# A hybrid convolution, pooling and MLP block on eight cores: layer norm output and MLP input transposed by DMA, Silu from side buffers, three gate products issued first, the last output tile in three column parts

## What is computed

```python
u = rms_norm(h, mix_pre_g)
proj = u @ w_in                                    # 1024 -> 5120
a, gate = split(proj[..., :2048]);  c = a * sigmoid(gate)
c = depthwise_causal_conv(c, dw_kernel, dw_bias)   # width 31
c = layer_norm(c, ln_g, ln_b)                      # over the 1024 channels of a token
y_conv = swish(c) @ w_conv_out
y_pool = pooling_branch(proj[..., 2048:3072])      # trailing means, per-group linear, w_pool_out
g_conv, g_pool = split(sigmoid(proj[..., 3072:]))
merged = g_conv * y_conv + g_pool * y_pool
h = h + rms_norm(merged @ w_o, mix_post_g)
v = rms_norm(h, mlp_pre_g)
v = square(relu(v @ w_ff1)) @ w_ff2                # 1024 -> 4096 -> 1024
h = h + rms_norm(v, mlp_post_g)
```

## Time and profile before

| | us |
|---|---|
| the three timed runs | 979.9, 981.34, 1103.43 |
| their median | 981.34 |
| the profiled execution | 980.87 |
| its span on its slowest core (core 7) | 979.3 |
| spans of all eight cores | 976.0 to 979.3 |

### The profile page before, as it was taken

One profiled execution on the slowest core, in us unless ns is written; L12 is line 12 of the kernel. 1 busy time (PEld: TensorE's weight loads), 2 busy tenths in 40 slices (PEclk: granted clock), 3 DMA queues, 4 the chain that ended last, 5 costly groups with the idle time before them and its releaser, 6 DMA issues.

```text
span 979.3 us, 15429 instructions; the slowest of 8 cores (976.0 to 979.3 us)
## 1 busy us (share of the span) xinstructions
PE 960.4 (98%) x5246; PEld 491.7 (50%) x5246; DVE 413.8 (42%) x671; ACT 338.3 (35%) x606; POOL 34.8 (4%) x50
## 2 busy tenths in 40 slices
PE   5999999999999999999999999999999999999997
PEld 3555666776554544444444444444444444444443
DVE  3464233334558213565555542254323542245222
ACT  3565223112112861464554331034211431034211
POOL 3000000000000000010101000000000000000000
PEclk9999999999999999999999999999999999999999
DMA  9999403656669008739597991340131301330021
GB/s 193 215 218 180 69 1 53 108 93 101 109 110 198 2 8 143 130 103 222 139 204 166 201 192 44 87 131 20 34 103 59 109 22 44 83 111 23 1 83 68
DMA packets 62175, 102.33 MB, mean 104 GB/s; under 512 B 10353, under 2 KB 42353, under 8 KB 62098
## 3 DMA queue, kind: packets, MB, share of 16 engines
q0 software_dynamic: 32608, 46.45, 31.8%
q1 hardware_dynamic: 24880, 53.31, 17.4%
q10 hardware_dynamic: 4610, 1.58, 0.6%
HBM read 127.78 MB, written 16.84 MB: 148 GB/s over the span
## 4 chain that ended last, share of the span: by engine, by line
PE 97%; DMA 1%; DVE 1%; ACT 0%; issue 0%; DVEq 0%; SPq 0%; ACTq 0%
PE ps L329 95%; PE ps L332 2%; DMA arena<-xh 1%; DVE arena L362 0%; ACT junkb L342 0%; DVE xb L352 0%; ACT arena L342 0%; DVE arena L352 0%; DVEq L173 0%; DVE tmpA L345 0%; SPq L365 0%; DVE sm L356 0%; ACT sm L342 0%; DVEq L140 0%; ACTq L140 0%
## 5 line engine op out<-in xcount | busy, mean ns | idle before, releaser
L329 PE MATMUL ps<-arena 128*128 128x512 bf16 (+2 forms) x4528 | 915.9, 364 | 4.1 <-DVE arena L362 2.9
L329 PEld LDWEIGHTS ps<-arena 128*128 128x128 bf16 x4528 | 450.2, 104 | 456.8 <-issue 6.1
L342 ACT ACTIVATE tmpA<-ps 128x512 f32<-128x512 f32 x226 | 133.3, 595 | 298.8 <-PE ps L329 264.6
L345 DVE TENSOR_TENSOR arena<-tmpA 128x512 bf16<-128x512 f32 x128 | 86.6, 691 | 77.7 <-ACT tmpA L342 77.6
L345 DVE TENSOR_TENSOR arena<-ps,tmpA 128x512 bf16<-128x512 f32 x64 | 43.9, 690 | 147.0 <-ACT tmpA L342 127.8
L342 ACT ACTIVATE junkb<-ps 128x512 bf16<-128x512 f32 x64 | 38.2, 597 | 163.2 <-DVE tmpA L345 108.5
L342 ACT ACTIVATE junkb<-arena 128x1024 bf16<-128x1024 f32 (+1 forms) x33 | 34.7, 1053 | 98.6 <-DMA arena<-xb 87.9
L342 ACT ACTIVATE arena<-ps 128x512 bf16<-128x512 f32 (+2 forms) x68 | 43.5, 651 | 52.5 <-PE ps L329 32.6
L356 DVE RECIPROCAL sm<-sm 128x1 f32<-128x1 f32 (+1 forms) x65 | 10.3, 159 | 107.6 <-ACT sm L342 107.1
L345 DVE TENSOR_TENSOR tmpA<-ps,gbt 128x512 f32<-128x512 f32 x64 | 44.1, 688 | 20.5 <-PE ps L329 19.6
L352 DVE SCALAR_TENSOR_TENSOR arena<-tmpA,sm,arena 128x1024 f32<-128x1024 f32 (+1 forms) x33 | 41.2, 1252 | 24.8 <-DMA arena<-out 20.5
(11 more groups left out here) (43 smaller groups left out, 196.0 us busy)
## 6 DMA issues: line engine op xcount, KB each, us to landing
arena<-xh SPq DMA_DIRECT2D x32, 512.0 KB, 9.6
arena<-w_ff POOLq DMA_DIRECT2D x16, 1024.0 KB, 25.4
out<-arena SPq DMA_DIRECT2D x31, 512.0 KB, 3.0
arena<-convw POOLq DMA_DIRECT2D x16, 768.0 KB, 6.6
arena<-out SPq DMA_DIRECT2D x16, 512.0 KB, 3.8
arena<-out SPq DMA_DIRECT2D x48, 128.0 KB, 3.8
arena<-w_in POOLq DMA_DIRECT2D x4, 1024.0 KB, 67.7
arena<-w_in POOLq DMA_DIRECT2D x2, 2048.0 KB, 23.2
```

What stands on the lines that cost most here:

```text
L329: kb.op("pe", lambda e: e.matmul(out_ap, lhsT=lhsT, rhs=rhs, start=start, stop=stop, skip_group_check=skip), reads=reads, writes=writes)
L342: kb.op("act", lambda e: e.activation(out=out_ap, in_=in_ap, func=func, **kw), reads=reads, writes=writes)
L345: kb.op(eng, lambda e: e.tensor_tensor(out=out_ap, in0=in0, in1=in1, op=op), reads=reads, writes=writes)
```

## The change

Five things differ:

- `cv_t3(cc)` issues DMA transposes from SP (`DTR`) instead of TensorE transposes: the 128 x 2048 slice `ru[:, cc, :]` goes block by block into one of four side buffers `t3v[cc % 4]`. The fourth is in two pieces, so a column with cc % 4 == 3 takes two DMAs. Two buffers lie where `xt[0]` and `xt[1]` are, the others in `xb` and in a piece at OFF_C + 12288. The Silu has moved to `cv_silu(cc)`, which reads the side buffer: one activation of 2048 elements, or two of 1024 for cc % 4 == 3.
- The order around it: `side2` is interleaved with groups 12 to 19. The transposes of columns 0 to 3 are issued ahead of group 20, those of 4 and 5 behind the Silu of columns 0 and 1, those of 6 and 7 behind the Silu of 2 and 3. A pair of Silus is issued behind each of groups 23, 26, 29 and 31.
- `gate_conv` is split into a gate part and a product part. In block 0 the gates of columns 0 to 2 are issued ahead of the first product, and from then on each gate is two columns ahead, with four `tmpA` buffers in place of two.
- `h_transp` is one DMA transpose of 128 x 1024 from `xb` into `hT`, for all 16 tiles. In blocks 1 to 3 it takes the place of `s6_transp` and `s6_spread`; `s6_load` reads one whole tile of 128 tokens with one DMA. `hT` is laid out as 8 x 512, so a matmul reads 512 elements in a row.
- The last tile is made by `last_tile`: its 1024 columns in parts of 512, 256 and 256, each with its square, multiply and partial sum, and the two halves of the result are stored from SP and from ACT.

Left out below are the removal of `next_xb`, of the list of source keys in `norm_part` and of the last tile's branch in `resid_b`, and the call of `s6_load(4 * blk + 4)`.

```diff
@@ -211,7 +211,10 @@
         wgc = aview(OFF_C, 8192, k=8, n=1024)
         XT_OFF = [OFF_C + 8192, OFF_C + 10240, OFF_S + 4096, OFF_S + 6144]
         xt = [aview(o, 2048).bitcast(F32) for o in XT_OFF]
-        hT = aview(OFF_S, 4096, s=16, k=8, t=32)
+        t3v = [[aview(XT_OFF[0], 2048, r=16, m=128)], [aview(XT_OFF[1], 2048, r=16, m=128)],
+               [xb[:, 0:2, :].rearrange("p b (r m) -> p (b r) m", m=128)],
+               [xb[:, 2, :].rearrange("p (r m) -> p r m", m=128), aview(OFF_C + 12288, 1024, r=8, m=128)]]
+        hT = aview(OFF_S, 4096, k=8, t=512)
         pwf = arena[:, OFF_Z:OFF_Z + Z_N].bitcast(F32).rearrange("p (k t) -> p k t", k=8)[:, :, 0:256]
         pws = xb[:, 0:2, :].rearrange("p b (k n) -> p (b k) n", k=4)
 
@@ -257,14 +260,15 @@
         kb.reg("wgc", (OFF_C, 8192))
         for b in range(4):
             kb.reg(("xt", b), (XT_OFF[b], 2048))
-            kb.reg(("hTp", b), (OFF_S, 4096))
-            kb.reg(("xq", b), (XT_OFF[0], 2048))
-        HT = [("hT", x, q, c) for x in range(4) for q in range(4) for c in range(4)]
-        for k in HT:
-            kb.reg(k, (OFF_S, 4096))
-        kb.disjoint(HT)
-        kb.disjoint([("hTp", b) for b in range(4)])
-        kb.disjoint([("xq", b) for b in range(4)])
+            kb.reg(("hT", b), (OFF_S, 4096))
+        kb.disjoint([("hT", b) for b in range(4)])
+        kb.reg(("t3", 0, 0), (XT_OFF[0], 2048))
+        kb.reg(("t3", 1, 0), (XT_OFF[1], 2048))
+        kb.reg(("t3", 3, 1), (OFF_C + 12288, 1024))
+        kb.reg(("t3", 2, 0), (ARENA_N, 2048))
+        kb.reg(("t3", 3, 0), (ARENA_N + 2048, 1024))
+        for b in range(3):
+            kb.reg(("xb", b), (ARENA_N + b * 1024, 1024))
         for h in range(2):
             kb.reg(("xth", h), (XT_OFF[1] + h * 1024, 1024))
         kb.disjoint([("utm", h, r) for h in range(2) for r in range(16)])
@@ -364,6 +368,9 @@
         def DMA(eng, out_ap, in_ap, reads, writes, after=()):
             return kb.op(eng, lambda e: e.dma_start(out=out_ap, in_=in_ap), reads=reads, writes=writes, dma=True, after=after)
 
+        def DTR(out_ap, in_ap, reads, writes):
+            return kb.op("sp", lambda e: e.dma_start(out=out_ap, in_=in_ap, transpose=True), reads=reads, writes=writes, dma=True)
+
         def wload(sl_ap, src_ap, keys, after=()):
             return DMA("pool", sl_ap, src_ap, [], keys, after=after)
 
@@ -677,14 +679,18 @@
                [("nr", r)], s2=rsd[:, 1, r:r + 1], op1=ALU.mult)
 
         def cv_t3(cc):
-            bb = (nb(), nb())
-            for r in range(16):
-                psb = ps[:, bb[r // 8], :].bitcast(BF16)
-                TR(psb[:, (r % 8) * 128:(r % 8 + 1) * 128], ru[:, cc, r * 128:(r + 1) * 128], identb[:], [("nr", r), "identb"], [PSK(bb[r // 8])])
+            i = cc % 4
+            for h in range(2 if i == 3 else 1):
+                n = 8 if i == 3 else 16
+                DTR(t3v[i][h], ru[:, cc, h * n * 128:(h + 1) * n * 128], [("nr", r) for r in range(16)], [("t3", i, h)])
+
+        def cv_silu(cc):
+            i = cc % 4
             sv = ru[:, cc, :].rearrange("p (m r) -> p m r", r=16)
-            for half in range(2):
-                ACT(sv[:, :, 8 * half:8 * half + 8], ps[:, bb[half], :].bitcast(BF16).rearrange("p (r m) -> p m r", r=8), AF.Silu,
-                    [PSK(bb[0]), PSK(bb[1]), "vec"], [("s", cc)], bias=vcol(8, cc), scale=vcol(0, cc))
+            for h, t in enumerate(t3v[i]):
+                n = 16 // len(t3v[i])
+                ACT(sv[:, :, h * n:(h + 1) * n], t.rearrange("p r m -> p m r"), AF.Silu,
+                    [("t3", i, k) for k in range(len(t3v[i]))] + ["vec"], [("s", cc)], bias=vcol(8, cc), scale=vcol(0, cc))
 
 
         def gate_pool(blk, cc):
@@ -700,19 +706,35 @@
             TTOP("dve", zt[:, cc, blk * 512:(blk + 1) * 512], ps[:, by, :], tmpA[:, t_i, :], ALU.mult,
                  [PSK(by), ("tmpA", t_i)], [("m1", blk, cc)])
 
-        def gate_conv(blk, cc):
-            bg, by = nb(), nb()
+        def gate_conv_g(blk, cc):
+            bg = nb()
             for kc in range(8):
                 MM(ps[:, bg, :], wgc[:, kc, cc * 128:(cc + 1) * 128], uT[:, kc, blk * 512:(blk + 1) * 512], kc == 0, kc == 7,
                    ["uT", "wgc"], [PSK(bg)])
+            t_i = nti(4 if blk == 0 else 2)
+            ACT(tmpA[:, t_i, :], ps[:, bg, :], AF.Sigmoid, [PSK(bg)], [("tmpA", t_i)])
+            return t_i
+
+        def gate_conv_y(blk, cc, t_i):
+            by = nb()
             for kc in range(8):
                 MM(ps[:, by, :], S[1][:, kc, cc * 128:(cc + 1) * 128], ru[:, kc, blk * 512:(blk + 1) * 512], kc == 0, kc == 7,
                    [("s", kc), "wco"], [PSK(by)])
-            t_i = nti(2)
-            ACT(tmpA[:, t_i, :], ps[:, bg, :], AF.Sigmoid, [PSK(bg)], [("tmpA", t_i)])
             m1 = zt[:, cc, blk * 512:(blk + 1) * 512]
             TTOP("dve", tmpA[:, t_i, :], ps[:, by, :], tmpA[:, t_i, :], ALU.mult, [PSK(by), ("tmpA", t_i)], [("tmpA", t_i)])
             TTOP("dve", m1, tmpA[:, t_i, :], m1, ALU.add, [("tmpA", t_i), ("m1", blk, cc)], [("m1", blk, cc)])
+
+        gate_ahead = []
+
+        def gate_conv(blk, cc):
+            if blk == 0:
+                if cc == 0:
+                    gate_ahead.extend(gate_conv_g(0, c) for c in range(3))
+                elif cc < 6:
+                    gate_ahead.append(gate_conv_g(0, cc + 2))
+                gate_conv_y(0, cc, gate_ahead.pop(0))
+            else:
+                gate_conv_y(blk, cc, gate_conv_g(blk, cc))
 
 
         DMA("sp", gb[:, 1, :], gbd[4:5, :].partition_broadcast(128), [], [("gb", 1)])
@@ -777,20 +799,27 @@
 
         side2 = [lambda q=q: ln_a(range(4 * q, 4 * q + 4)) for q in range(4)] + [ln_rstd] + \
                 [lambda q=q: ln_b(range(4 * q, 4 * q + 4)) for q in range(4)]
-        interleave(groups[12:21], side2)
+        interleave(groups[12:20], side2)
 
         def t3_pair(i):
             cv_t3(2 * i)
             cv_t3(2 * i + 1)
 
+        def silu_pair(i):
+            cv_silu(2 * i)
+            cv_silu(2 * i + 1)
+
         DMA("sp", gb[:, 1, :], gbd[1:2, :].partition_broadcast(128), [], [("gb", 1)])
         DMA("sp", gb[:, 0, :], gbd[2:3, :].partition_broadcast(128), [], [("gb", 0)])
-        for i in range(4):
-            groups[21 + 2 * i]()
-            t3_pair(i)
-            groups[22 + 2 * i]()
-        for f in groups[29:]:
-            f()
+        t3_pair(0)
+        t3_pair(1)
+        for n in range(20, 32):
+            groups[n]()
+            if n in (23, 26, 29, 31):
+                i = (n - 22) // 3
+                silu_pair(i)
+                if i < 2:
+                    t3_pair(i + 2)
         wload(S[2][:, :, :], wo_v, ["wo"])
 
         def ff1_load(c):
@@ -837,8 +859,8 @@
             DMA("sp", xt[j % 4], xmain[j], [], [("xt", j % 4)])
 
         def h_transp(j, bi):
-            transp_part(128, bi, lambda b, psb: COPY(
-                alt(), hT[:, 4 * j:4 * j + 4, :, :], psb.rearrange("p (k s t) -> p s k t", k=8, s=4), [PSK(b)], [("hTp", j)]))
+            tl = j % 4
+            DTR(hT[:, :, tl * 128:(tl + 1) * 128], xb[:, bi, :], [("xb", bi)], [("hT", tl)])
 
         e_pend = []
 
@@ -875,39 +897,49 @@
         ff2_load(1, 2)
 
 
-        def s6_load(blk, x):
-            for q in range(4):
-                DMA("sp", xt[0][32 * q:32 * q + 32, :], omain[4 * blk + q][32 * x:32 * x + 32, :], [("outh", 4 * blk + q)], [("xq", q)])
+        def s6_load(j):
+            DMA("sp", xt[0], omain[j], [("outh", j)], [("xt", 0)])
 
         def s6_norm():
-            return norm_part(128, xt[0], [("xq", q) for q in range(4)], 0)
-
-        def s6_transp(x, bi):
-            bo = next_xb()
-            kb.op("dve", lambda e: e.transpose(xb[:, bo, :].rearrange("p (c k t) -> p k c t", c=4, k=8),
-                                               xb[:, bi, :].rearrange("p (k c t) -> p k c t", k=8, c=4)),
-                  reads=[("xb", bi)], writes=[("xb", bo)])
-            return bo
-
-        def s6_spread(x, bo):
-            for q in range(4):
-                for c in range(4):
-                    DMA(("sp", "act")[c % 2], hT[32 * c:32 * c + 32, 4 * q + x, :, :].rearrange("p k t -> p (k t)"), xb[32 * q:32 * q + 32, bo, 256 * c:256 * c + 256],
-                        [("xb", bo)], [("hT", x, q, c)])
-
-        def ff1_unit(fc, hkeys):
+            return norm_part(128, xt[0], ("xt", 0), 0)
+
+        def ff1_unit(fc):
             b = nb()
             c, fl = fc // 4, fc % 4
             wv = ff1_view(c)
             for kc in range(8):
-                MM(ps[:, b, :], wv[:, kc, fl * 128:(fl + 1) * 128], hT[:, :, kc, :], kc == 0, kc == 7,
-                   [("ff1", c)] + (hkeys if kc in (0, 7) else []), [PSK(b)])
+                MM(ps[:, b, :], wv[:, kc, fl * 128:(fl + 1) * 128], hT[:, kc, :], kc == 0, kc == 7,
+                   [("ff1", c)] + [("hT", t) for t in range(4)], [PSK(b)])
             t_i = nti(2)
```

(64 more changed lines are left out.)

## The result

| | before | changed |
|---|---|---|
| median of all timed runs, us | 981.12 | 984.99 |
| profiled execution, us | 980.87 | 984.87 |
| its span, us | 979.3 (core 7) | 983.3 (core 2) |

Now and then cores run at a lower granted clock and an execution takes longer (1170.88 us in one of the changed kernel's seven); such executions are in the medians but not in the ratios and their intervals. The ratio of changed to before is 1.0038, with a 95% interval from 1.0028 to 1.0048. The changed kernel is 0.4% slower: the same by the bound of 2%, but clear of noise and on the wrong side of the forecast of 973.2 us. It lies inside the stated range.

A forecast was written before the change was run, and what follows sets the result against it. TensorE, busy 98% of the span, was taken as the bound: 980.87 - 7.16 - 1.79 (transposes) - 0.3 (tail) + 0.1 (256-column parts) + 1.5 (stall) = 973.2 us. Its own range was 971 to 976 us, the wider one 969 to 990 us.

The forecast's parts named there:

- What bounds the kernel, and what is removed: TensorE, busy 98% of the span, bounds the kernel; removing transposes of cv_t3 (7.16 us) and h_transp (1.79 us) gains 8.95 us.
- When ACT wants them: Block 0's Silus: pairs start at 334.5, 344.9, 355.2 and 363.9 us, 2.45 us per Silu of 2,048; last ends 368.8 us.
- the stall of 1.5 us: TensorE's wait at block 0's first product for column 7's Silus, 0.9 to 1.9 us, taken as 1.5 us.
- Rival C: ACT becomes the bound: Silu from the side buffer at half speed, four turns some 22 us late, 995 us; chance 0.04.
- The window for the DMA transposes: Before the first product: layer norm transposes cost no more than ACT's own stall up to 5.5 us per 512 KB column.
- The price of a DMA transpose: One 512 KB column of the layer norm's output takes 3 to 5 us and stays hidden.
- Rivals A and B: DMA transposes of a column too slow: A above 9 us, 1020.0 us, chance 0.12; B 5.5 to 9 us, chance 0.13.
- the mechanism of 1309 ns a block: Extreme of A: DMA transposes block by block, about 21 us a column, 1097 us in all; 4 in 100 of A's 12.
- Work moved with it, and the tail: Moved loads and 256 KB transposes cost nothing below about 7 us each; the last tile's tail gains 0.3 us.

The follow-up runs named there:

- The last version: Changed kernel with Silu in place in a row, DVE copy permuting into token order, and six gates ahead of the first product: 971.75 us, ratio 0.9905.

## Why the prediction was wrong

**What bounds the kernel, and what is removed: right.** The 8.95 us of transposes come back in full as soon as nothing waits. The last version gains 9.0 us by the medians of its session (980.75 and 971.75 us) and 8.9 us on the chain.

**When ACT wants them: the step that failed.** I priced the Silu of 2,048 "at two of the old, 2.45 us" and bounded it between 2.11 and 2.45 us. It took 3.87 us and more. Both bounds were taken from rows that don't do what the new instruction does: a strided read from PSUM, and a read in a row from SBUF. Each of these is quick, and the combination, strided from SBUF, is in neither. The trace of before couldn't price it, so nothing supported an upper bound of 2.45 us. The rule was to be had in the Trainium skill. Advanced Engine Details and Errata, section Memory Cachelines, says that accesses that each fall on a new 16-byte line of SBUF are penalised, and that at least two hits on a line are needed. The trace agrees for ScalarE's read, 1.89 ns against 1.02 ns an element. Whether DVE pays too isn't shown: its walking copy of 1,024 elements took 1.04 us and its in-place layer norm of 1,024, in runs of 128, 0.54 us, but no run has the same copy in a row.

The rest of that step held. From the first pair's start to the last Silu's end I had 368.8 - 334.5 = 34.3 us, and it took 373.86 - 330.12 = 43.7 us, 9.4 us more. The first two turns (11.9 and 12.4 us) ran 1.5 and 2.0 us over their three groups, the third took 11.4 us where I had 8.66 us, and the last pair 8.0 us instead of 4.9 us. With the stall of 1.5 us that I had taken this makes 10.9 us; 10.3 us for Silus and 0.9 us for DVE were measured.

**The rival that came true had 0.04.** Rival C, ACT becomes the bound, was the right mechanism, down to Silu at half speed. Its time of 995 us was too high. It took 9.8 us for a pair instead of 7.7 to 8.1 us, and its 22 us were added up wrongly: with turns of some 14 us the last Silu ends at about 386 us, 17 us later than 368.8 us, which makes 991 us. I argued it away with "the walk from PSUM now has the same step". That sentence is the error: the same step in another memory is not the same price.

**A slip that cost nothing by itself.** The row at 322.16 us is the end of group 21, not of group 20: the first pair of `cv_t3` follows groups[21]. All groups came 3.45 us earlier than I wrote, and so did the Silus that follow them. The wait at the first product is a difference between the two and stays. The window for the DMA transposes shrinks from 5.5 to 5.1 us a column.

**The price of a DMA transpose: right, and the least of the worries.** I took 3 to 5 us. The first two, of 512 KB each, took 4.5 us (median) from issue to landing; the groups that mix 512 and 256 KB have 4.0 and 4.3 us. In sequence it is less. On SP's queue the first two occupy 5.6 us and the next two (512 and 256 KB) 3.8 us:

```profile
320.65 5.60 SPq L372 DMA_TRANSPOSE arena<-arena  x2
326.35 3.78 SPq L372 DMA_TRANSPOSE xb<-arena  x2
330.21 9.46 SPq L372 DMA_TRANSPOSE arena<-arena  x3
```

The first was issued at 320.65 us. The forecast was 321.6 us, or 320.5 us with the 1.06 us of the earlier start. Rivals A and B fall with it. So does the mechanism of 1309 ns a block, the figure of the Trainium skill (VectorE: DVE Perf Modes, The three transpose paths): by it the estimate for 16 blocks was 20.9 us, and the trace has 4.5 us. The 261 GB/s that the prediction cites from the Trainium skill (DMA: Bandwidth & Descriptors, Latency and other measured facts) is near what the trace has: 212 GB/s on average from 326 to 330 us, when only these transposes were in flight. I gave A and B 0.25 of the chances, six times what I gave to C, because the unknown operation caught my eye and the known one in a new place did not.

**What I left out altogether: the clock.** The prediction priced a wait at its length. Behind waits of 2.1 us, of 3.8 us and of 6.7 and 3.6 us in a row came 3 to 6 us of matmuls at half clock, 1.5 to 3 us more.

**Work moved with it, and the tail: right or nearly.** TensorE never waits for `hT` or for weights. Under weight loads a DMA transpose of 256 KB took up to 19.3 us to land, more than the 7 us that I had set as the limit, and even that was covered. The tail from the last matmul to the end went from 5.87 to 5.80 us; I had 0.3 us less, too much. The 256-column parts cost what was said.

## What to carry to other kernels

When a change moves an operation from PSUM to SBUF, or from one engine to another, price its access pattern there anew. A row that has the memory and a row that has the stride don't bound the row that has both. If an engine's turn is close to the time that covers it (8.66 us under 10.4 us here), errors in its price add up turn by turn and are paid at the end of the stage. Look for the engine that is idle in that stage: here DVE made the walk for half of ScalarE's price and, with six gates ahead, off the path.

Issuing independent matmuls ahead of a product that must wait was worth nearly the TensorE time moved: 3.2 us of waiting for 3.45 us, and 5.1 us (6.5 us less the new wait of 1.4 us) for 5.2 us.

## What the runs showed of the hardware

- ScalarE, Silu on 128 x 2048 bf16 in SBUF: 2.09 us in a row on both sides, 3.87 us with reads 256 bytes apart, 9.05 us with writes 32 bytes apart. From PSUM the same 256-byte step cost no more than a row from SBUF: 1.20 us for 1,024, against 1.23 us.
- DVE, copy of 128 x 2048 bf16 in SBUF with reads 256 bytes apart: 1.98 us. What it takes in a row was not run.
- TensorE with its moving operand in runs of 32 elements (64 bytes) keeps its pace (49 in 10.74 us, as elsewhere). With single elements 256 bytes apart the matmuls of that stage averaged 0.62 us, and the granted clock was 0.63 with TensorE busy throughout.
- DMA transposes between SBUF regions: two of 512 KB landed in 4.5 us (median) with nothing beside them, sixteen of 256 KB in 5.6 us (median, at most 19.3 us) beside other traffic. One occupies SP's queue for 1.2 to 5.7 us.
- The granted clock was at 0.50 when TensorE restarted behind waits of 0.8 and 2.1 us in a row, of 3.8 us, and of 6.7 and 3.6 us in a row, and was back at 1.00 some 3, 6 and 5 us later. It stayed at 1.00 behind a single wait of 1.2 us, and behind 1.4 and 1.1 us nine us apart.
